# Expert routing on VectorE: choosing per tile, ordering the experts by a matmul, finding a row's slot as one number

## What is computed

```
glog = x @ w_group + b_group;  g = argmax(glog);  pg = softmax(glog)[g]
elog = x @ w_expert + b_expert                       # 4 groups of 8 experts
vals, loc = top_k(elog[g], 2);  gates = pg * softmax(vals);  eid = g * 8 + loc
# the 2T assignments are sorted by expert, padded to blocks, and each block of rows goes through
hb = silu(xb @ w_gate[e]) * (xb @ w_up[e]);  y = hb @ w_down[e]
# and y * gate is added up per token
```

## Time and profile before

| | |
|---|---|
| median of 3 runs | 2393.61 us (2393.48 to 2396.33) |
| profiled execution, its own time | 2393.96 us |
| its span, first to last instruction | 2392.1 us |
| busy in the span | PE 2159.3 us (90%), VectorE 712.2 (30%), ScalarE 527.4 (22%), GpSimd 303.4 (13%) |
| DMA | 545.90 MB, mean 228 GB/s |
| mean granted TensorE clock | 0.947 |

### The profile page before, as it was taken

How to read it: one execution, slowest core, us unless ns; L and a number is a source line. 1 busy time by engine, 2 the same in 40 slices (tenths; PEclk the granted TensorE clock), 3 DMA queues, 4 the chain that set the end, 5 groups by cost and what they waited for, 6 DMA issues and landing times. The chain is left out here.

```text
span 2392.1 us, 28466 instructions
## 1 busy us (share of the span) xinstructions
PE 2159.3 (90%) x11566; PEld 1234.4 (52%) x11566; DVE 712.2 (30%) x1554; ACT 527.4 (22%) x1219; POOL 303.4 (13%) x313
## 2 busy tenths in 40 slices
PE   7999989999999999968999999959996899999991
PEld 3446744444444588345555555547754555555550
DVE  1044325442664445352101101142125211011104
ACT  2123121022554144112121121130001222112111
POOL 0000000211232311101111111022000111111101
PEclk9999998999999999978999999979997899999996
DMA  9315233132003121138999999971133899999993
GB/s 345 133 39 181 81 142 123 43 133 71 1 1 110 70 92 53 47 141 336 424 423 424 423 424 423 412 271 53 71 114 115 338 422 422 424 423 422 422 413 124
DMA packets 100632, 545.90 MB, mean 228 GB/s; under 512 B 13360, under 2 KB 27481, under 8 KB 66554
## 3 DMA queue, kind: packets, MB, share of 16 engines
q1 hardware_dynamic: 79766, 495.65, 51.3%
q0 software_dynamic: 20384, 48.01, 5.6%
q10 hardware_dynamic: 340, 0.28, 0.0%
HBM read 538.79 MB, written 28.94 MB: 237 GB/s over the span
## 5 line engine op out<-in xcount | busy, mean ns | idle before, releaser
L727 PE MATMUL ps<-arena,ring 128*128 128x512 f32 (+11 forms) x2000 | 609.4, 464 | 10.6 <-DVE arena L2112 2.2
L727 PEld LDWEIGHTS ps<-arena,ring 128*128 128x128 f32 (+3 forms) x2000 | 359.0, 190 | 248.9 <-issue 205.6
L1176 PE MATMUL ps<-ring,arena 128*64 128x256 f32 x3648 | 411.9, 383 | 4.3 <-ACT arena L1598 3.2
L1176 PEld LDWEIGHTS ps<-ring,arena 128*64 128x64 f32 x3648 | 258.2, 138 | 137.6 <-ACT arena L1598 4.0
L808 PE MATMUL ps<-ring,arena 128*128 128x512 f32 (+1 forms) x560 | 249.4, 603 | 6.5 <-DVE arena L2103 4.2
L1189 PE MATMUL ps<-ring,arena 128*64 128x512 f32 x896 | 213.0, 619 | 21.1 <-DMA ring<-in_moe_w_down_dram 21.1
L2253 DVE SCALAR_TENSOR_TENSOR arena<-arena,ps 128x256 f32<-128x256 f32 x78 | 32.9, 421 | 562.6 <-ACT arena L1608 562.6
L2526 POOL DMA_INDIRECT assignment_rows<-arena x78 | 82.0, 1052 | 810.2 <-ACT arena L1614 782.0
L808 PEld LDWEIGHTS ps<-ring,arena 128*128 128x128 f32 (+1 forms) x560 | 102.5, 187 | 140.4 <-issue 140.1
L1176 PE MATMUL ps<-arena 128*64 128x256 f32 x1344 | 151.1, 380 | 0.0
L1189 PEld LDWEIGHTS ps<-ring,arena 128*64 128x64 f32 x896 | 66.3, 143 | 135.3 <-issue 104.2
(11 more groups left out here) (313 smaller groups left out, 1863.4 us busy)
## 6 DMA issues: line engine op xcount, KB each, us to landing
ring<-in_moe_w_gate_dram SPq DMA_DIRECT2D x48, 2048.0 KB, 22.9
ring<-in_moe_w_up_dram SPq DMA_DIRECT2D x48, 2048.0 KB, 26.2
ring<-in_moe_w_down_dram SPq DMA_DIRECT2D x48, 2048.0 KB, 21.2
arena<-in_moe_w_gate_dram SPq DMA_DIRECT2D x16, 2048.0 KB, 23.5
arena<-in_moe_w_up_dram SPq DMA_DIRECT2D x16, 2048.0 KB, 25.0
arena<-in_moe_w_down_dram SPq DMA_DIRECT2D x16, 2048.0 KB, 26.1
ring<-in_ada_w_dram SPq DMA_DIRECT2D x12, 2048.0 KB, 11.9
ring<-in_a_w_in_dram SPq DMA_DIRECT2D x12, 1536.0 KB, 14.9
```

Source lines behind the costliest of these rows:

```text
L727: ins = pe.matmul(dst, w, m, start=i == 0, stop=i == len(pairs) - 1)
L1176: ins = pe.matmul(ps[CAP * i:CAP * (i + 1), bank_, 256 * j:256 * (j + 1)], rows_t[:, k, :], w[:, k, 256 * i:256 * (i + 1)], start=k == 0, ...
```

## The change

- **Choice per tile.** A new function `choose` makes the choice for one tile: eleven operations on 128x8 and 128x32 operands, each waiting for the one before, but for the two one-hots, which go together. `finish_and_turn` calls it for tiles whose logits are there, at the end of the turn of a later tile, and for the last two tiles after the last copy: the third tile's choice ahead of the last tile's logits, the last tile's behind them. `route` starts with the difference of logits for the gates.
- **Mask.** Multiply, make the offset and add become one subtract-compare and one multiply-add.
- **Order.** The 32x1024 comparison and its sum give way to: pick each expert's own key onto its partition (multiply with the identity and reduce, 32x32), compare it with all keys (32x32, bf16), raise `above_ready`; a new PE job "order" multiplies that by ones, and its product, copied from PSUM, is the rank on every partition.
- **Place.** Row and block become one slot number, 64 x block + row: one tile A, one product with both one-hots (128 x 2 x 160), one reduction, then a conversion to integers, a mask and a shift, and a conversion back.
- **Gates.** Their four operations move behind the one-hots of the table.
- **Table.** PE adds an outer product of ones and a row of 4096 first; assignments are numbered from -4096. The table then needs no marking by VectorE: one conversion, and the two shifts that the gathers need, come directly behind it.
- For the second layer, four tiles are handled where five were.

```diff
-    return j + [f"router{l}_{order[-1]}", f"ranks{l}", f"table{l}"]
+    return j + [f"router{l}_{order[-1]}", f"ranks{l}", f"order{l}", f"table{l}"]
...
+                pe.wait_ge(above_ready, l + 1)
+                b0, _ = begin(f"order{l}")
+                end(product(b0[:, 0:NE], [(ones_h[0:NE, :], above[0:NE, :])]))
...
+                pe.wait_ge(numbers_set, 9)
+                pe.matmul(b0[:, 0:NBLK], ones[0:1, :], empty_row, start=True, stop=False)
...
                     if late and i < len(order) - 1:
+                        pending.append(late[0])
                         logits(late.pop(0))
                     normalise(k - 1, t)
                     for s in late:
                         logits(s)
+                        pending.append(s)
                     if hold and i == 2:
                         turn_copy(k, order[1])
+                    while pending and i < len(order) - 1:
+                        choose(pending.pop(0))
                 turn_copy(k, order[-1])
                 if logits:
+                    for s in pending:
+                        choose(s)
                     logits(order[-1])
+                    choose(order[-1])
...
+                def tile(t):
+                    r = rows_of(t)
+                    taken(vec, f"router{l}_{t}")
+                    settle()
+                    step(vec.max(g8[:, t, :], lg[:, t, 0:8]))
+                    step(vec.max_index(gi8[:, t, :], g8[:, t, :], lg[:, t, 0:8]))
+                    step(vec.tensor_copy(sm[:, 1, t:t + 1], gi8[:, t, 0:1]))
+                    step(vec.tensor_scalar(tq[:, t, :], group_of[:], sm[:, 1, t:t + 1], 1.0, ALU.is_equal, ALU.subtract))
+                    step(vec.scalar_tensor_tensor(elm[:, t, :], tq[:, t, :], -NEG, lg[:, t, 8:40], ALU.mult, ALU.add))
+                    step(vec.max(e8[:, t, :], elm[:, t, :]))
+                    step(vec.max_index(ei8[:, t, :], e8[:, t, :], elm[:, t, :]))
+                    step(vec.tensor_copy(sm[:, 2:4, t], ei8[:, t, 0:2]))
+                    for k in range(2):
+                        mark(vec.tensor_scalar(oh[:, k, t, :], expert_of[:], sm[:, 2 + k, t:t + 1], None, ALU.is_equal))
+                    settle()
+                    ins = vec.tensor_tensor(ohb[0:r, t, :], oh[0:r, 0, t, :], oh[0:r, 1, t, :], ALU.add)
...
-                mark(vec.tensor_tensor(compared, spread(key, 1, NE), spread(key, 2, NE), ALU.is_gt))
-                mark(vec.tensor_scalar(ci, ci, 6, None, ALU.arith_shift_right))
-                mark(vec.tensor_reduce(rank, compared, AX.X, ALU.add))
+                mark(vec.tensor_tensor(key_col[0:NE], key[0:NE], ident[0:NE, 0:NE], ALU.mult))
+                mark(vec.tensor_reduce(cnt[0:NE, 1, 0:1], key_col[0:NE], AX.X, ALU.add))
+                vec.tensor_scalar(above[0:NE], key[0:NE], cnt[0:NE, 1, 0:1], None, ALU.is_lt).then_inc(above_ready, 1)
+                done(vec, f"order{l}")
+                free(vec.tensor_copy(rank, job_bank(f"order{l}", NE)), f"order{l}")
...
+                step(vec.tensor_tensor(picked[:, :, 0:nt, :], oh[:, :, 0:nt, :], spread(A, 1, 2), ALU.mult))
+                step(vec.tensor_reduce(slot_of[:, 0:nt, :].rearrange("p t k -> p k t"), picked[:, :, 0:nt, :], AX.X, ALU.add))
+                step(vec.tensor_copy(slot_i[:, 0:2 * nt], slots[:, 0:2 * nt]))
+                mark(vec.tensor_scalar(place_i[:, 0:2 * nt], slot_i[:, 0:2 * nt], CAP - 1, None, ALU.bitwise_and))
+                mark(vec.tensor_scalar(place_i[:, 10:10 + 2 * nt], slot_i[:, 0:2 * nt], 6, None, ALU.arith_shift_right))
+                step(vec.tensor_copy(place, place_i))
...
-                step(vec.tensor_scalar(emptied, job_bank(name, NBLK), 0.0, float(EMPTY), ALU.is_equal, ALU.mult))
-                free(vec.scalar_tensor_tensor(emptied, job_bank(name, NBLK), -1.0, emptied, ALU.add, ALU.add), name)
-                mark(vec.tensor_copy(slot_tok, emptied))
+                step(vec.tensor_copy(slot_tok, job_bank(name, NBLK)))
...
+            pool.memset(empty_row, float(EMPTY)).then_inc(numbers_set, 1)
```

More of the change, by code:

```diff
@@ L60 @@
 NBLK = NBS + NOVER
-EMPTY = 1 << 20
+EMPTY = 1 << 12
 ALPHA = 4.0 ** 0.25
@@ L396, in build @@
         cnt = at(RT + 1120, 4 * NE).rearrange("p (n e) -> p n e", e=NE)
-        key, rank, heavy, base_of, need, over_at = (at(23936 + NE * i, NE) for i in range(6))
+        key, key_col, heavy, base_of, need, over_at = (at(23936 + NE * i, NE) for i in range(6))
         need_i = at(23936 + NE * 6, NE).bitcast(I32)
-        rank_i = at(24160, 5 * NE).bitcast(I32).rearrange("p (t n) -> p t n", n=NE)
-        row_of = at(R0, 10).rearrange("p (t k) -> p t k", k=2)
-        block_of = at(R0 + 16, 10).rearrange("p (t k) -> p t k", k=2)
+        full = at(24160, NE)
+        above = at(24160 + NE, NE // 2).bitcast(BF16)
+        slot_i = at(24160 + 2 * NE, 10).bitcast(I32)
+        place_i = at(24160 + 3 * NE, 20).bitcast(I32)
+        rank = at(24160 + 4 * NE, NE)
+        slot_of = at(R0 + 20, 10).rearrange("p (t k) -> p t k", k=2)
+        place = at(R0, 10 * 2)
         picked = at(R0 + 32, 2 * 5 * NE).rearrange("p (k t n) -> p k t n", k=2, n=NE)
-        blk = at(R0 + 352, 5 * NE).rearrange("p (t n) -> p t n", n=NE)
         emptied = at(R0 + 7168, NBLK)
         row_hot = at(R0 + 576, 10 * P).rearrange("p (i r) -> p i r", r=P)
-        compared = at(R0 + 576, NE * NE).rearrange("p (a b) -> p a b", b=NE)
         block_hot = at(R0 + 1856, 10 * NBLK).rearrange("p (i b) -> p i b", b=NBLK)
@@ L1745, in turn_copy, with finish_and_turn @@
                 ins.then_inc(turn_copied[1], 1)
-            def finish_and_turn(k, order, finish, logits=None, hold=False):
-                after = routers_after(order, hold)
+            def finish_and_turn(k, order, finish, logits=None, choose=None, hold=False):
+                after, pending = routers_after(order, hold), []
                 for i, t in enumerate(order):
@@ L2125, in _ @@
             clear_routing()
-            finish_and_turn(3, (4, 0, 1, 2, 3), lambda t, h: residual(2, t, f"outC_{t}", h), logits(0), hold=True)
+            finish_and_turn(3, (4, 0, 1, 2, 3), lambda t, h: residual(2, t, f"outC_{t}", h), logits(0), choose(0, (4, 0, 1, 2, 3)), hold=True)
             def route(l):
-                tiles = range(5 if l == 0 else 4)
-                taken(vec, f"router{l}_2")
-                taken(vec, f"router{l}_3")
+                nt = 5 if l == 0 else 4
+                mark(vec.tensor_tensor(adr[:, 0:nt, 0:NG], lg[:, 0:nt, 0:NG], spread(g8[:, 0:nt, 0], 2, NG), ALU.subtract))
@@ L2133, in route @@
                 settle()
[L2134 to L2162, removed]
-                    mark(vec.tensor_tensor(ohb[0:META, 4, :], oh1[0:META, 4, :], oh2[0:META, 4, :], ALU.add))
@@ L2208, in route @@
                 step(vec.tensor_scalar(need, need, 1.0, 0.0, ALU.subtract, ALU.max))
-                step(vec.tensor_tensor_scan(cnt[:, 2, :], need, cnt[:, 3, :], 0.0, ALU.add, ALU.add))
+                mark(vec.tensor_tensor_scan(cnt[:, 2, :], need, cnt[:, 3, :], 0.0, ALU.add, ALU.add))
+                free(vec.tensor_tensor(T_, c, spread(full, 1, nt), ALU.is_ge), name)
+                taken(vec, name)
+                settle()
                 step(vec.tensor_tensor(need, cnt[:, 2, :], need, ALU.subtract))
@@ L2211, in route @@
                 step(vec.tensor_tensor(over_at, need, over_at, ALU.subtract))
[L2212 to L2216 removed]
+                step(vec.scalar_tensor_tensor(T_, T_, float(CAP), spread(over_at, 1, nt), ALU.mult, ALU.mult))
@@ L2367, in _ @@
             clear_routing()
-            finish_and_turn(5, range(NT), lambda t, h: residual(4, t, f"outD_{t}", h), logits(1))
+            finish_and_turn(5, range(NT), lambda t, h: residual(4, t, f"outD_{t}", h), logits(1), choose(1, range(NT)))
             route(1)
```

73 lines of the change are left out of this document (33 added, 40 removed).

## The result

| | before | changed |
|---|---|---|
| median, same chip (range; 5 runs each) | 2393.61 us (2393.39 to 2397.91) | 2380.33 us (2379.98 to 2382.20) |
| profiled execution | 2393.96 | 2379.99 |
| its span | 2392.1 | 2378.3 |
| mean granted clock | 0.947 | 0.951 |

The ratio is 0.9941 (0.9929 to 0.9953): 0.6% faster. The sum was made against the profiled execution and came to a gain of 13.9; that execution gained 13.97, the median 13.3. The busy times hardly moved (PE 2159.5, VectorE 712.5, ScalarE 525.8, GpSimd 304.3): the gain is idle time of PE ahead of the two expert stages.

A forecast was written before the change was run, and what follows sets the result against it. It took VectorE's serial routing chain to delay both expert stages, whose pace the weights set. Stages starting 7.25 and 6.65 us earlier, limited by the gathers, sum to 13.9: 2393.96 - 13.9 = 2380.1, range 2375.5 to 2385.0.

The forecast's parts named there:

- The forecast case: Whole kernel: both routings shorten and both expert stages start earlier, a gain of 11 to 16 us, likeliest 2380; chance 0.70.
- Choice: Start of each routing: only the last tile's choice stays behind its logits, 2.5 us; gain 4.7 and 4.6.
- Early choices hidden: VectorE ahead of the routings: seven other choices of 2.5 us each fit its idle time, taken at nothing.
- The rival of exposed choices: Early choices on VectorE delay PE, up to 17.5 us, giving 2397.6; chance 0.03.
- Order: Ranking of experts in the routing: 3.55 us falls to 1.8; gain 1.75, and 1.7 in the second routing.
- the round trip: VectorE to PE's order product and back: taken as 0.43 us, between nothing and 0.81.
- To SyncE's order: From the ranking to the experts' order for SyncE: 1.56 us falls to 1.17; gain 0.4 and 0.3.
- Places: Behind SyncE's order, ahead of the table's one-hots: 3.8 us falls to 3.65; gain 0.15, second routing 0.1.
- Gather: First row gathers share DMA with slabs 6 and 7; they land 7.25 and 6.65 us earlier, less than the tokens gain.
- Block 0's clock: Start of each expert stage: 9.07 us stays; rival, low clock throughout, 14.2, loses 5.1 per layer, 2390.3; chance 0.04.
- Steps that cost little: Rival: waits in the new chains cost little, last choice 1.2 us instead of 2.5, gain 16.5, 2377.5; chance 0.08.
- The rival of full waiting: Gathers wait fully for weights, or slab 6 meets earlier loads: up to 2 us less per layer, 2384.0; chance 0.12.

The follow-up runs named there:

- the ten added ones: Changed kernel with ten more short dependent steps in the last tile's choice, ahead of the order: median 2386.28 us, ratio 0.9957.
- PE kept busy: Changed kernel with 28 throwaway identity transposes on PE before the first gather's wait: 2377.28 us, ratio 0.9925; with slab 7 also behind the gather: 2376.14, 0.9913.
- the second run with slab 7 held back: Changed kernel with slab 7 loaded only after the first gather landed, rerun beside the changed kernel: median 2379.08 us, ratio 0.9923.

## Why the prediction was right

The forecast case came: 2380.1 was said by the sum and 2380.3 measured, with the gain by the same stretches and for the same reason. By its steps:

- **Choice.** 2.5 was said, 2.51 measured; gain 4.7 and 4.6 as said. The kernel with the choice put back, 9.5 for 9.3, confirms it alone.
- **Early choices hidden.** 48.08 against 48.09 us: nothing was paid. Made twice, they cost 4.3 of 17.5. The rival of exposed choices falls, but its mechanism is real, and the margin was the 1.32 us that one more choice overran.
- **Order.** The mis-sized term: the round trip took 0.29, not 0.43, and the part 1.67, not 1.8. That was inside its bounds (nothing and 0.81), nearer to the lower. The ranks' own wait went from 0.81 to 0.82, so the gates were rightly taken as hidden there.
- **To SyncE's order.** 1.19 / 1.15 left, gain 0.37 / 0.31 (0.4 and 0.3 said). **Places** 3.65 (3.65 said). The table's one-hots as before, gates hidden with 0.36 and 0.18 us to spare, behind the table 0.61 (0.62 said).
- **Gather.** The step that mattered most for the path: it let the sum take 7.25 and 6.65 where the tokens came 7.69 and 7.36 earlier. 7.19 and 6.92 were measured. The second was under-sized: its least time from slab 6 to the transposes had been set at 13.5, and 13.38 was measured (13.73 in the first). The reason given, two slabs of 9.9 us at 423 GB/s, was too short: in the trace of before slab 7 lands 12.6 behind its issue, 13.0 behind slab 6's, so it shares the DMA engines with the first gather too (issued 9.99 behind slab 6), and the two slabs' 4.2 MB went at some 320 GB/s, not 423.
- **What the part behind the order is worth.** The tokens gained 7.69 and the order 7.00; the transposes 7.19. So 0.69 / 0.58 of gain behind the order (places, table) passed on 0.19 / 0.14, and the last step, the marking product, nothing that can be told. The prediction's sum of small gains behind the order (0.62 / 0.57) was right as length and mostly worthless as time, which its gather step said (0.4 and at most 0.1).
- **Block 0's clock.** The 9.07 was to stay; 9.27 and 9.10. The rival (14.2) fell. The next load, not the transposes, carries the gain on, so block 0's 0.20 / 0.15 more is paid. The step had block 0's length fixed, when it depends on when the clock rises (below).
- **Steps that cost little.** A dependent step is 0.203 in the ten added ones, and the last choice 2.51 for thirteen instructions. At the 0.09 of independent ones it would have been 1.2. The Trainium skill ("VectorE: DVE Perf Modes", The DRAIN you can't avoid) says of eight copies, 13.88 us either way, that a semaphore after each costs nothing extra. The trace doesn't bear that out for instructions as short as these, and that rival fell.
- **Gathers and weights.** The rival of full waiting fell as a size, but the runs show the mechanism: with slab 7 or both held back the gather takes 3.67 to 3.88 to the transposes. With both on their way it takes the longer the sooner it follows slab 6: 3.72 at 11.48 us, 3.92 at 9.99, 4.41 at 9.32, 5.21 at 8.17 (up to 5.45 elsewhere, and 6.29 once with PE kept busy). The Trainium skill agrees ("DMA: Bandwidth & Descriptors", Issuing engines are not separate DMA queues: transfers issued by different engines share the same sixteen and interleave).

The case held some luck: errors of a few tenths of both signs (the round trip and the second gather better than said, block 0 0.20 and 0.15 worse) cancelled to 0.1.

## What to carry to other kernels

In a stage that runs in gapless small dependent steps ahead of a busy one, count links times 0.2 us, and move out of it whatever has its inputs earlier; check the idle place that takes it in against the length of the moved piece, as a second piece in the same place was paid for. Ask of each saved microsecond which transfer or clock it will meet next: here those ahead of the order were kept nearly whole (by the transposes 9.3 of 9.3, 2.6 of 2.7 and 3.6 of 4.1 us), and of the 0.69 and 0.58 that the change saved behind it a quarter. When PE has waited long ahead of a busy stretch, try throwaway products in that wait: they brought the next loads 3.6 us forward here, where rows 0.7 and 1.4 us earlier brought them at most 0.9.

## What was not expected of the hardware

- **Block 0 differs from run to run.** In every trace but the two with PE kept busy, its same 64 products took between 8.66 and 10.10 us (24 cases), against 7.13 at clock 1.00, so the low clock cost 1.5 to 3.0 at each start. Each time it was, within 0.07, 7.13 and half of the time from its start to the rise of the clock, which was 3.1 to 6.1 us: 4.4 in the changed kernel's first routing made 9.27, 6.1 in the first routing of the second run with slab 7 held back made 10.10. That is why single distances scatter: with the choice put back, the transposes came 4.50 and 4.84 later, block 0 took 8.73 and 9.81, and the next load came 3.96 and 5.54 later. The six cases with slab 7 held back had 9.39 to 10.10, but other kernels' second routings had up to 9.91 too. What sets the moment of the rise stays open.
- **A PE product asked for by VectorE and read back by it costs 0.29 us** between the two VectorE instructions (one of 32 columns in bf16, at clock 0.50).
- **A gather that waits longer lands faster.** Issued 2.15 us later, its rows were turned only 0.73 later in the second routing.
